# Starting the high parts of the weights 4 and 248 bytes further in two of four ring slots

## The chip, the cores and the metric

The kernel runs on one core of a Trainium2 chip. The metric is the device time of one execution in microseconds, the median of several runs. The kernel before took 1588.19 us (three runs, 1588.19 to 1588.33).

## What is computed

One layer of a streaming encoder block on a 256 x 2048 float32 input: a normed input is multiplied by `w_in` (2048 x 7680), the product feeds a gated spatial branch and a windowed attention branch, both go through output projections and `w_o`, and a gated MLP with a short causal convolution follows.

```
h = rms_norm(x, ln_pre_mix);  proj = h @ w_in
y_a = gmlp_branch(u, v_sg, ...) @ w_a_out;  y_b = swa_branch(q, k, v, ...) @ w_b_out
x = x + rms_norm((gate_a * y_a + gate_b * y_b) @ w_o, ln_post_mix)
up = rms_norm(x, ln_pre_ffn) @ w_up                    # 2048 x 16384
x = x + rms_norm((gelu(conv(gate)) * conv(val)) @ w_down, ln_post_ffn)
```

## The kernel before

Every large product is made from split operands. A float32 value is written as a high part (rounded to the type `F32R`) and a low part (what the rounding left), and three of the four products of the parts are summed: high by high, high by low and low by high.

**The flow of weights.** SyncE loads 1 MB units of weights into `raw` (four units of 2048 columns per partition). Each unit is two halves of 1024 columns. ScalarE rounds a half into `w_hi` (`split`, L454) and VectorE writes the rest into `w_lo` (`split`, L862). Both tensors are rings of four slots, and half h of a turn uses slot h modulo 4. ScalarE may overwrite a slot once TensorE has counted the half up on `half_used`; TensorE starts on a half once `hi_ready` or `lo_ready` says so.

**Two kinds of stages.** In the feature-major stages the weights are the stationary operand and the activations in `actT` the moving one. These are q, k, v and u, the gates, the two branch outputs, and the up-projection. A half has eight blocks of 128 x 128 weights. `by_hi` (L1494) loads a block of the high part and multiplies it with 512 columns (both parts of 256 tokens); `by_lo` (L1498) loads the same block of the low part and multiplies it with 256 columns (the high part alone). I call the first a wide matmul and the second a narrow one. `pair_a` works through two halves: 16 wide and 16 narrow matmuls. In `group_turn` the pairs alternate: halves 0 and 1 go wide first, then narrow; halves 2 and 3 go narrow first (`lo_first`), then wide. So a block of 64 matmuls reads, by slot: wide 0, wide 1, narrow 0, narrow 1, narrow 2, narrow 3, wide 2, wide 3, and then wide 0 again. There are 88 such blocks, in 44 turns. In `y_turn` (8 blocks of 64) every pair goes wide first. In the other stages (`half_b`, L1585, `half_v`, L1635, `last_halves`, L1598, and `seven_products`, L1778) the weights or forms of them are the moving operand. The first turn of the up-projection reads the high parts through `half_a` (L1509 and L1514), which the change leaves at the start of the slot.

**Where the parts lie.** A slot of `w_hi` is 1024 columns (4096 bytes per partition), and each of its blocks starts at a multiple of 512 bytes from the tensor's start. A slot of `w_lo` is 1152 columns (4608 bytes) wide, and in the feature-major stages the low part begins 64, 32, 16 and 128 bytes into slots 0 to 3 (`LO_SHIFT`, in columns 16, 8, 4, 32). `actT` comes behind them, and each of its rows begins at a multiple of 2048 bytes from its own start.

Of the kernel before, what the change touches and what calls it, by code (L numbers as in the profile page):

```python
# [6 lines left out]
ALU = mybir.AluOpType  # L7
ACT = mybir.ActivationFunctionType
AX = mybir.AxisListType
F32 = mybir.dt.float32  # L10
F32R = mybir.dt.float32r

P = 128
# [22 lines left out]
HALF = UNIT // 2  # L36
RAW = 4
RING = 4
# [24 lines left out]
def block_program(nc, x, x_t, pre_gains, w_in, ln_v_g, ln_v_b, w_spatial, b_spatial, rel_bias, sinks, w_a_out, w_b_out,  # L63
# [10 lines left out]
    with ExitStack() as ctx:  # L74
        def sb(name, shape, dt=F32):
            return ctx.enter_context(nc.sbuf_tensor(name, shape, dt))

        def sem(name):
            return ctx.enter_context(nc.semaphore(name))


        raw = sb("raw", [P, RAW, UNIT])
        w_hi = sb("w_hi", [P, RING, HALF], F32R)
        w_lo_padded = sb("w_lo", [P, RING, HALF + P], F32R)
        w_lo = w_lo_padded[:, :, 0:HALF]
        LO_SHIFT = (16, 8, 4, 32)
        w_lo_shifted = [w_lo_padded[:, slot, shift:shift + HALF] for slot, shift in enumerate(LO_SHIFT)]
# [93 lines left out]
        ps = ctx.enter_context(nc.psum_tensor("ps", [P, 8, 512], F32))  # L181
# [17 lines left out]
        hi_ready = sem("hi_ready")  # L199
        lo_ready = sem("lo_ready")  # L200
# [242 lines left out]

        @block.scalar
        def _(act):
            def split(m, h, fresh=False, free=None):

                if fresh and h == 2:
                    act.wait_ge(third_half_landed, 16)
                else:  # L450
                    act.wait_ge(raw_landed[h // 2], 16 * m + 16)
                if not fresh:
                    act.wait_ge(half_used, 8 * m + (h - RING + 1 if free is None else free))
                act.activation(w_hi[:, h % RING, :], raw[:, h // 2, h % 2 * HALF:(h % 2 + 1) * HALF], ACT.Copy)\  # L454
                   .then_inc(hi_ready, 1)

            def split_xs(m, h, src, free=None):

                act.wait_ge(half_used, 8 * m + (h - RING + 1 if free is None else free))
                act.activation(xs[:, h % RING, 0, :], src, ACT.Copy)  # L460
                split(m, h, free=free)

            def copy_out(g, bank, used):
                act.wait_ge(half_used, used)
# [4 lines left out]
            def split_x(k):  # L469
                for i, (k0, k1) in enumerate(XPIECES):  # L470
                    if k0 == k:
                        act.wait_ge(x_landed[i], 16)
                act.activation(actT[:, k, 0, :], xT[:, k, :], ACT.Copy, scale=gvec[:, 0, k:k + 1]).then_inc(hi_split, 1)
# [21 lines left out]
            def square(src, junk, col, done_sem=None):  # L495
                act.activation(junk, src, ACT.Square, accum_out=stat[:, col:col + 1]).then_inc(sq_done, 1)

            def root(col, t, before):
                act.wait_ge(ms_done, before + t + 1)
                act.activation(stat[:, ROOT + col + t:ROOT + col + t + 1], stat[:, col + t:col + t + 1], ACT.Sqrt)\  # L500
                   .then_inc(rt_done, 1)
# [17 lines left out]
            act.wait_ge(small["gains"], 16)  # L519
            for h in (2, 3):  # L520
                split_x(h)
                split(0, h, fresh=True)


            for h, k in ((4, 4), (5, None), (6, 6), (7, None)):
                if k is not None:
                    split_x(k)
                    split_x(k + 1)
                split(0, h)
            for h, k in ((0, 8), (1, 10), (2, 12), (3, 14), (4, None), (5, None), (6, None), (7, None)):  # L530
                if k is not None:
                    split_x(k)
                    split_x(k + 1)
                split(1, h)
                if h in (3, 4):
                    act.wait_ge(x_rows_landed, 16)
                    if h == 4:
                        act.wait_ge(sq_done, 1)
                    square(xn[:, h - 3, :], xs[:].rearrange("p r a s -> p (r a s)"), MIX_IN + h - 3)
                if h == 5:  # L540
                    for t in range(T):
                        root(MIX_IN, t, 0)

            for i in range((N_U - N_QKV) // 8):
                m = i + N_QKV // 8
# [34 lines left out]
            m = N_U // 8  # L580
# [166 lines left out]
            for i in range(2):  # L747
                m = N_WO // 8 + 2 + i
# [10 lines left out]
            m = N_UP // 8  # L759
# [8 lines left out]
            act.wait_ge(half_used, N_UP)  # L768
            square(ps[:, 3, :], junk_mix[:, T + 1, 512:SW], LAST_SQ[0])
            root(MIX_OUT, 1, 2 * T)  # L770
            split(m, 2)
            split_first_rows(1, 0, 1)
            split(m, 3)
            split_rows(1, 4, 1)
            split(m, 4)
            split(m, 5)
            split_rows(1, 4, 2)
            split(m, 6)
            act.wait_ge(x1_done, T * (D // XC - 1) + 2)
            square(x1[:, 0, :], junk_x1[:, 0, :], FFN_IN)  # L780
            split_rows(1, 4, 3)
            split(m, 7)
            act.wait_ge(x1_done, T * (D // XC) + 1)
            square(x1[:, 1, :], junk_x1[:, 1, :], FFN_IN + 1)
            for t in range(T):
# [69 lines left out]

        @block.vector
        def _(dve):
            def split(m, h, shifted=True):

                dve.wait_ge(hi_ready, 8 * m + (h + 1))  # L860
                lo = w_lo_shifted[h % RING] if shifted else w_lo[:, h % RING, :]
                dve.tensor_tensor(lo, raw[:, h // 2, h % 2 * HALF:(h % 2 + 1) * HALF],  # L862
                                  w_hi[:, h % RING, :].bitcast(F32), ALU.subtract).then_inc(lo_ready, 1)

            def split_xs(m, h, src):

                dve.wait_ge(hi_ready, 8 * m + (h + 1))
                dve.tensor_tensor(xs[:, h % RING, 1, :], src, xs[:, h % RING, 0, :].bitcast(F32), ALU.subtract)
                split(m, h, shifted=False)

            def add_out(g, bank, dst):
                dve.wait_ge(copied, g + 1)
# [59 lines left out]
            for k in (0, 1):  # L932
                dve.wait_ge(x_landed[k], 16)
                dve.tensor_scalar(actT[:, k, 0, :], xT[:, k, :], gvec[:, 0, k:k + 1], None, ALU.mult).then_inc(first_hi, 1)
                if k == 0:
                    split_x(0)
                    split(0, 0, shifted=False)
            split_x(1)
            split(0, 1, shifted=False)
            for h in (2, 3):  # L940
                split_x(h)
                split(0, h, shifted=False)
            for h, k in ((4, 4), (5, None), (6, 6), (7, None)):
                if k is not None:
                    split_x(k)
                    split_x(k + 1)
                split(0, h, shifted=False)
            for h, k in ((0, 8), (1, 10), (2, 12), (3, 14), (4, None), (5, None), (6, None), (7, None)):
                if k is not None:
                    split_x(k)  # L950
                    split_x(k + 1)
                split(1, h, shifted=False)
                if h == 4:
                    for t in range(T):
                        mean_square(MIX_IN, D, t, sq_done, t + 1)
                if h == 5:
                    for t in range(T):
                        recip(MIX_IN, t, 0)
                        col = RECIP + MIX_IN + t
                        dve.tensor_copy(rrep[:, t, :], stat[:, col:col + 1].broadcast_to([P, P])).then_inc(rrep_done, 1)  # L960
                if h == 6:
                    dve.wait_ge(small["relb"], 16)
                    dve.tensor_copy(relperm[0:BUCKETS].rearrange("p (k a b) -> p k a b", a=2, b=2),
                                    relb[:].rearrange("p (k b a) -> p k a b", a=2, b=2)).then_inc(rb_perm, 1)
# [4 lines left out]
            for i in range((N_U - N_QKV) // 8):  # L969
                m = i + N_QKV // 8  # L970
# [28 lines left out]
            m = N_U // 8  # L999
# [271 lines left out]
            for i in range(2):  # L1271
                m = N_WO // 8 + 2 + i
# [11 lines left out]
            m = N_UP // 8  # L1284
# [50 lines left out]
            residual(1, 1)  # L1335
            last_out(1, x1[:, 1, SW:D], gain[:, SW:D], sq_done, 4 * T + 1)
            split_rows(1, KD + 2, 1)
            split(m, 2, shifted=False)
            split(m, 3, shifted=False)
            residual(2, 0)  # L1340
            residual(2, 1)
            split_rows(1, KD + 2, 2)
            split(m, 4, shifted=False)
            residual(3, 0)
            residual(3, 1)
            split(m, 5, shifted=False)
            split_rows(1, KD + 2, 3)
            split(m, 6, shifted=False)
            split(m, 7, shifted=False)
            for t in range(T):  # L1350
                mean_square(FFN_IN, D, t, sq_done, 4 * T + t + 2)
            for t in range(T):
# [138 lines left out]
        @block.tensor  # L1491
        def _(pe):
            def by_hi(h, at, k, c, bank, start, stop):
                return pe.matmul(ps[:, bank + c, :], w_hi[:, h % RING, at:at + P],  # L1494
                                 actT[:, k, :, :].rearrange("p a s -> p (a s)"), start=start, stop=stop)

            def by_lo(h, at, k, c, bank, start, stop):
# [338 lines left out]
            m = N_UP // 8  # L1836
# [88 lines left out]
```

## Time and profile before

| | |
|---|---|
| median of the runs | 1588.19 us |
| the profiled execution, its own time | 1588.61 us |
| its span, first to last instruction | 1586.8 us |
| TensorE matmul busy | 1577.7 us, 99% |
| TensorE weight load busy | 1367.8 us, 86% |
| VectorE busy | 1260.4 us, 79% |
| ScalarE busy | 828.1 us, 52% |
| granted TensorE clock, mean | 0.999 |

A matmul's busy time runs past the start of the next one, since they are pipelined. The time that a matmul costs is therefore read as the step from its start to the start of the next. In the chain of work that ended last, consecutive matmuls of one line stand as one piece with its duration and their number, and duration over number is the mean step. Durations there have two decimals, so a piece is known to about 10 ns.

### The profile page before, as it was taken

Reading aid. Unit: us, or ns where it says so; the run is one execution under the profiler, and the core shown is the slowest. Engines: PE = TensorE matmul, PEld = TensorE weight load, DVE = VectorE, ACT = ScalarE, POOL = GpSimd, SP = SyncE. Lnnn points to the kernel's source line nnn. Section 1 sums busy time; section 2 is a strip of 40 time slices with the busy share of each in tenths; the row PEclk is TensorE's granted clock in tenths of the full one; section 3 lists DMA queues with packets and bytes.
Section 4 is the critical chain, followed back from the end, with each engine's and each line's share of the span. In section 5 each row is a group of like instructions: output and inputs, shape, how many; then the busy total and the mean of one; then the engine's idle time right before and its main releaser. Section 6 shows DMA issues by size and latency. Waiting matters only on the chain.

```text
span 1586.8 us, 24342 instructions
## 1 busy us (share of the span) xinstructions
PE 1577.7 (99%) x8652; PEld 1367.8 (86%) x8652; DVE 1260.4 (79%) x1836; ACT 828.1 (52%) x1124; POOL 1.9 (0%) x12
## 2 busy tenths in 40 slices
PE   9999999999999999999999999999999999999998
PEld 8888888888888888888888888888888888888886
DVE  6556677677797788777787777877778899989999
ACT  6544544456565654444444444444444575766664
POOL 0000000000000000000000000000000000000000
PEclk9999999999999999999999999999999999999999
DMA  9895455556566465556555566655666555555552
GB/s 371 267 232 190 160 185 163 181 160 203 194 241 217 152 210 187 186 185 200 190 190 185 185 197 190 195 185 185 195 189 198 199 208 207 208 198 200 185 212 106
DMA packets 234946, 313.15 MB, mean 197 GB/s; under 512 B 5360, under 2 KB 209808, under 8 KB 234000
## 3 DMA queue, kind: packets, MB, share of 16 engines
q1 hardware_dynamic: 231056, 306.44, 58.5%
q10 hardware_dynamic: 3840, 6.05, 1.5%
q8 instruction: 32, 0.52, 0.1%
q14 instruction: 18, 0.15, 0.0%
HBM read 309.58 MB, written 2.88 MB: 197 GB/s over the span
## 4 chain that ended last, share of the span: by engine, by line
PE 96%; DVE 4%; issue 0%; ACT 0%; DVEq 0%
PE ps L1494 44%; PE ps L1498 23%; PE ps L1585 15%; PE ps L1778 6%; PE ps L1635 3%; PE ps L1598 1%; DVE actT L1189 1%; DVE w_lo L1189 1%; PE ps L1509 1%; PE ps L1514 0%; DVE arena L1177 0%; PE ps L1724 0%; PE ps L1705 0%; PE ps L1657 0%; PE ps L1717 0%
## 5 line engine op out<-in xcount | busy, mean ns | idle before, releaser
L1494 PE MATMUL ps<-actT,w_hi 128*128 128x512 f32 x3072 | 715.4, 390 | 0.0
L454 ACT ACTIVATE w_hi<-raw 128x1024 fp32r<-128x1024 f32 x420 | 433.4, 1056 | 509.0 <-PE ps L1494 256.9
L862 DVE TENSOR_TENSOR w_lo<-raw,w_hi 128x1024 fp32r<-128x1024 f32 x422 | 506.1, 1223 | 236.8 <-ACT w_hi L454 234.5
L1494 PEld LDWEIGHTS ps<-actT,w_hi 128*128 128x128 f32 x3072 | 569.4, 188 | 113.0 <-issue 0.2
L1498 PEld LDWEIGHTS ps<-actT,w_lo 128*128 128x128 f32 x3072 | 378.2, 188 | 9.9 <-issue 1.7
L1498 PE MATMUL ps<-actT,w_lo 128*128 128x256 f32 x3072 | 384.4, 281 | 0.0
L1585 PE MATMUL ps<-w_hi,xs 128*128 128x512 f32 x832 | 226.6, 389 | 0.0
L1585 PEld LDWEIGHTS ps<-w_hi,xs 128*128 128x128 f32 x832 | 156.1, 188 | 32.4
L1585 PE MATMUL ps<-w_lo,xs 128*128 128x512 f32 x416 | 128.1, 389 | 0.0
L1189 DVE TENSOR_TENSOR w_lo<-raw,w_hi 128x1024 fp32r<-128x1024 f32 x96 | 117.3, 1222 | 0.0
L1379 DVE SCALAR_TENSOR_TENSOR arena<-arena,convw 128x256 f32<-128x256 f32 x256 | 106.8, 480 | 0.0
L713 ACT ACTIVATE w_hi<-raw 128x1024 fp32r<-128x1024 f32 x96 | 100.4, 1046 | 0.0
L1585 PEld LDWEIGHTS ps<-w_lo,xs 128*128 128x128 f32 x416 | 78.1, 188 | 16.3
L1778 PE MATMUL ps<-actT 128*128 128x512 f32 x288 | 81.0, 389 | 0.1
L691 ACT ACTIVATE actT<-raw 128x1024 fp32r<-128x1024 f32 x24 | 25.4, 1060 | 99.0 <-PE ps L1778 99.0
L873 DVE TENSOR_TENSOR arena<-ps,arena 128x512 f32<-128x512 f32 (+1 forms) x106 | 72.5, 684 | 1.5 <-ACT arena L467 1.4
L1778 PE MATMUL ps<-actT,a_parts 128*128 128x512 f32 x216 | 64.6, 389 | 0.0
L1778 PEld LDWEIGHTS ps<-actT 128*128 128x128 f32 x288 | 54.0, 188 | 11.8 <-DVE actT L1189 0.6
L467 ACT ACTIVATE arena<-ps 128x512 f32<-128x512 f32 x106 | 61.3, 579 | 2.9 <-PE ps L1514 1.4
L1189 DVE TENSOR_TENSOR actT<-arena,actT 128x1024 fp32r<-128x1024 f32 (+2 forms) x52 | 59.8, 1161 | 0.0
L711 ACT ACTIVATE xs<-arena 128x256 fp32r<-128x256 f32 x96 | 38.7, 403 | 24.7 <-PE ps L1585 13.8
L1367 DVE TENSOR_TENSOR arena<-arena,rrow 128x512 f32<-128x512 f32 x64 | 44.3, 692 | 6.5
(181 smaller groups left out, 935.7 us busy)
## 6 DMA issues: line engine op xcount, KB each, us to landing
raw<-in_w_up_dram SPq DMA_DIRECT2D x128, 1024.0 KB, 5.5
raw<-in_w_down_dram SPq DMA_DIRECT2D x64, 1024.0 KB, 5.2
raw<-in_w_in_dram SPq DMA_DIRECT2D x58, 1024.0 KB, 5.2
raw<-in_w_o_dram SPq DMA_DIRECT2D x16, 1024.0 KB, 5.3
raw<-in_w_a_out_dram SPq DMA_DIRECT2D x8, 1024.0 KB, 5.3
raw<-in_w_b_out_dram SPq DMA_DIRECT2D x8, 1024.0 KB, 5.2
arena<-in_x_dram SPq DMA_DIRECT2D x1, 2048.0 KB, 17.1
arena<-in_x_dram ACTq DMA_DIRECT2D x2, 1024.0 KB, 6.1
```

Source lines behind the costliest of these rows:

```text
L454: act.activation(w_hi[:, h % RING, :], raw[:, h // 2, h % 2 * HALF:(h % 2 + 1) * HALF], ACT.Copy)\
L467: act.activation(lo_part, ps[:, bank:bank + 2, S:2 * S], ACT.Copy).then_inc(copied, 1)
L713: act.activation(w_hi[:, slot, :], raw[:, unit.slot, j * HALF:(j + 1) * HALF], ACT.Copy).then_inc(hi_ready, 1)
L862: dve.tensor_tensor(lo, raw[:, h // 2, h % 2 * HALF:(h % 2 + 1) * HALF], w_hi[:, h % RING, :].bitcast(F32), ALU.subtract).then_inc(lo_read ...
L873: dve.tensor_tensor(dst, ps[:, bank:bank + 2, 0:S], lo_part, ALU.add).then_inc(summed, 1)
L1189: return dve.tensor_tensor(lo, full, hi.bitcast(F32), ALU.subtract)
L1379: dve.scalar_tensor_tensor(out=dst[:, a, :], in0=src[:, a, i:i + S], scalar=w(i, a), in1=dst[:, a, :], op0=ALU.mult, op1=ALU.add).then_inc ...
L1494: return pe.matmul(ps[:, bank + c, :], w_hi[:, h % RING, at:at + P], actT[:, k, :, :].rearrange("p a s -> p (a s)"), start=start, stop=stop)
L1498: return pe.matmul(ps[:, bank + c, 0:S], w_lo_shifted[h % RING][:, at:at + P], actT[:, k, 0, :], start=start, stop=stop)
L1585: ins = pe.matmul(ps[:, bank + 2 * t + c, :], xpart[:, tokens], wpart[:, slot, c * 512:(c + 1) * 512], start=(first and xpart is x_hi and ...
L1635: ins = pe.matmul(ps[:, 4 + 2 * t + c, :], xpart[:, t * P:(t + 1) * P], wpart[:, slot, c * 512:(c + 1) * 512], start=(k == 0 and xpart is ...
L1778: ins = pe.matmul(ps[:, bank, :], x[x_part], y[y_part], start=(unit.first and alone and x_part + y_part == 0), stop=(unit.last and alone a ...
```

## The change

`w_hi` becomes 1152 columns wide per slot, like `w_lo`. In the feature-major stages the high part then begins at column 0, 0, 1 and 62 of slots 0 to 3, that is 0, 0, 4 and 248 bytes further on. ScalarE writes there, VectorE reads there, and TensorE loads its stationary blocks from there. All three address a half as 8 blocks of 128 columns, which is the same run of addresses as before. In the other stages, and for the first turn of the up-projection, everything stays at the start of the slot (`padded=False` for ScalarE, `feature_major=False` for VectorE, the new name of `shifted=False`). What is allocated behind `w_hi` moves by 2048 bytes, and slot n of `w_hi` by 512 n bytes.

```diff
-        w_hi = sb("w_hi", [P, RING, HALF], F32R)
+        w_hi_padded = sb("w_hi", [P, RING, HALF + P], F32R)
+        w_hi = w_hi_padded[:, :, 0:HALF]
+        HI_SHIFT = (0, 0, 1, 62)
+        w_hi_blocks = [w_hi_padded[:, slot, shift:shift + HALF].rearrange("p (b c) -> p b c", c=P)
+                       for slot, shift in enumerate(HI_SHIFT)]
...
-            def split(m, h, fresh=False, free=None):
+            def split(m, h, fresh=False, free=None, padded=True):
...
-                act.activation(w_hi[:, h % RING, :], raw[:, h // 2, h % 2 * HALF:(h % 2 + 1) * HALF], ACT.Copy)\
-                   .then_inc(hi_ready, 1)
+                full, hi = raw[:, h // 2, h % 2 * HALF:(h % 2 + 1) * HALF], w_hi[:, h % RING, :]
+                if padded:
+                    full, hi = full.rearrange("p (b c) -> p b c", c=P), w_hi_blocks[h % RING]
+                act.activation(hi, full, ACT.Copy).then_inc(hi_ready, 1)
...
-            def split(m, h, shifted=True):
+            def split(m, h, feature_major=True):
...
-                lo = w_lo_shifted[h % RING] if shifted else w_lo[:, h % RING, :]
-                dve.tensor_tensor(lo, raw[:, h // 2, h % 2 * HALF:(h % 2 + 1) * HALF],
-                                  w_hi[:, h % RING, :].bitcast(F32), ALU.subtract).then_inc(lo_ready, 1)
+                full, hi = raw[:, h // 2, h % 2 * HALF:(h % 2 + 1) * HALF], w_hi[:, h % RING, :].bitcast(F32)
+                lo = w_lo[:, h % RING, :]
+                if feature_major:
+                    full, hi = full.rearrange("p (b c) -> p b c", c=P), w_hi_blocks[h % RING].bitcast(F32)
+                    lo = w_lo_shifted[h % RING].rearrange("p (b c) -> p b c", c=P)
+                dve.tensor_tensor(lo, full, hi, ALU.subtract).then_inc(lo_ready, 1)
...
             def by_hi(h, at, k, c, bank, start, stop):
-                return pe.matmul(ps[:, bank + c, :], w_hi[:, h % RING, at:at + P],
+                return pe.matmul(ps[:, bank + c, :], w_hi_blocks[h % RING][:, at // P, :],
                                  actT[:, k, :, :].rearrange("p a s -> p (a s)"), start=start, stop=stop)
```

## Rows read from the trace of the kernel before

**Rows 1.** The page: busy time, share of the span, instructions, by engine.
```profile
PE 1577.7 (99%) x8652; PEld 1367.8 (86%) x8652; DVE 1260.4 (79%) x1836; ACT 828.1 (52%) x1124; POOL 1.9 (0%) x12
```

**Rows 2.** Waits of TensorE, 61 to 1244 us: engine line <- releaser: us, times, longest.
```profile
PE ps L1824 <- DVE arena L1295: 0.5, 1, 0.5
PE ps L1526 <- DVE actT L919: 0.4, 1, 0.4
```

**Rows 3.** Chain that ended last, up-projection: start us, us, engine line, matmuls.
```profile
1008.89 7.26 PE ps L1494 x32
1016.15 3.78 PE ps L1498 x32
1019.93 7.26 PE ps L1494 x32
...
1030.97 7.26 PE ps L1494 x32
```

**Rows 4.** The chain cut to short windows around one change from narrow to wide.
```profile
1009.80 2.27 PE ps L1494 x10
...
1027.66 0.35 PE ps L1498 x3
...
1030.97 0.69 PE ps L1494 x3
```

**Rows 5.** The chain where weights are the moving operand (both parts).
```profile
477.30 43.52 PE ps L1585 x192
...
1244.36 21.76 PE ps L1585 x96
```

**Rows 6.** The chain in the branch outputs, every pair wide first.
```profile
379.60 3.65 PE ps L1494 x16
383.24 1.88 PE ps L1498 x16
385.13 3.64 PE ps L1494 x16
```

**Rows 7.** Groups by line and shape: busy us, mean ns of one, idle before.
```profile
L1494 PE MATMUL ps<-actT,w_hi 128*128 128x512 f32 x3072 | 715.4, 390 | 0.0
L1494 PEld LDWEIGHTS ps<-actT,w_hi 128*128 128x128 f32 x3072 | 569.4, 188 | 113.0 <-issue 0.2
L454 ACT ACTIVATE w_hi<-raw 128x1024 fp32r<-128x1024 f32 x420 | 433.4, 1056 | 509.0 <-PE ps L1494 256.9 <-PE ps L1498 238.7 <-DMA raw<-in_w_in_dram 10.8
L713 ACT ACTIVATE w_hi<-raw 128x1024 fp32r<-128x1024 f32 x96 | 100.4, 1046 | 0.0
L661 ACT ACTIVATE actT<-arena 128x1024 fp32r<-128x1024 f32 x4 | 4.0, 1051 | 1.6 <-DVE arena L1032 1.6
L1379 DVE SCALAR_TENSOR_TENSOR arena<-arena,convw 128x256 f32<-128x256 f32 x256 | 106.8, 480 | 0.0
L896 DVE SCALAR_TENSOR_TENSOR actT<-arena,gvec,actT 128x256 fp32r<-128x256 f32 x16 | 7.2, 480 | 0.1
```

**Rows 8.** Timeline, all engines: start us, us, engine line, [idle before <- releaser].
```profile
1032.83 1.06 ACT L454 ACTIVATE w_hi<-raw 128x1024 fp32r<-128x1024 f32 x1 [2.64 <-PE ps L1494]
1033.92 1.23 DVE L862 TENSOR_TENSOR w_lo<-raw,w_hi 128x1024 fp32r<-128x1024 f32 x1 [1.93 <-ACT w_hi L454]
1034.64 1.06 ACT L454 ACTIVATE w_hi<-raw 128x1024 fp32r<-128x1024 f32 x1 [0.75 <-PE ps L1494]
...
1035.74 1.23 DVE L862 TENSOR_TENSOR w_lo<-raw,w_hi 128x1024 fp32r<-128x1024 f32 x1 [0.59 <-ACT w_hi L454]
...
1038.07 3.94 PE L1498 MATMUL ps<-actT,w_lo 128*128 128x256 f32 x32
```

**Rows 9.** The chain in the up-projection's first turn, no part shifted (`half_a`).
```profile
546.25 0.95 PE ps L1514 x8
547.20 1.84 PE ps L1509 x8
...
549.40 0.36 PE ps L1514 x3
```

**Rows 10.** The chain in the opening matmuls, plain float32, 128 columns.
```profile
2.85 2.35 PE ps L1657 x11
```

## What I expected before the kernel ran

> **What bounds the kernel now.** I began with the page's busy times: TensorE is busy for 99% of the span, VectorE for 79%, ScalarE for 52% [rows 1]. A busy share says little for a pipelined engine, so I asked next for TensorE's waits. Over all feature-major stages, 1183 us long, it waits for another engine for 0.9 us in total [rows 2]. What is left to look at is the steps of the matmuls themselves, and they come out of the chain of work that ended last. In the up-projection it is an unbroken alternation of 32 wide matmuls in 7.26 us and 32 narrow ones in 3.78 us; two blocks later the starts (1008.89, 1019.93, 1030.97) have moved by exactly 11.04 us each time [rows 3]. So one block of 64 costs 11.04 us whatever the other engines do. Only a change in the steps of the matmuls can move the end.
>
> The reader should then compare the steps. Where the weights are the moving operand, 192 matmuls take 43.52 us and 96 take 21.76 us: 226.67 ns each, both parts alike [rows 5]. This is the even step of a matmul of 512 columns here. In the up-projection ten wide matmuls in the middle of a run take 2.27 us, the same even step, while the first three behind a narrow run take 0.69 us [rows 4] instead of 3 x 226.67 ns = 0.68 us. The narrow ones go at 3.78 / 32 = 118.1 ns [rows 3], with 0.35 us for three inside slot 0 [rows 4]. In the up-projection's first turn, where no low part is shifted, three narrow matmuls in the middle of a half take 0.36 us, 120 ns each [rows 9]. So the start of the stationary block does matter to the step of a narrow matmul: 120 ns with none of the parts shifted, about 118 ns with the low part shifted. What it does to a wide matmul no row shows, since every high part begins at a multiple of 512 bytes.
>
> **The change part by part.** It removes and adds no instruction and no wait. Its effects are these.
>
> (1) The wide matmuls of slots 2 and 3 load their blocks from addresses 4 and 248 bytes on. There are 16 in each of 96 blocks of 64, 1536 in all. Their weight load has a mean of 188 ns [rows 7] against a step of 226.67 ns, so it lies beside the matmul before it, and it ends in time even if it grows somewhat. Only the first load of slot 2 lies beside a narrow matmul. What can go is the unevenness behind it: 0.69 - 0.68 = 0.01 us per block [rows 4, 5] in the 88 blocks that turn from narrow to wide at slot 2, 0.88 us. The eight blocks of the branch outputs turn to wide at slot 2 and at slot 0; their runs of 16 take 3.65 and 3.64 us [rows 6] against 16 x 226.67 ns = 3.63 us, so at slot 2 there is 8 x 0.02 = 0.16 us. Together 1.04 us, if all of it goes. As these differences are at the limit of the view's two decimals, the ends are 0 and twice that, 2.1 us.
>
> (2) The steady step of these 1536 matmuls. The nearest rows give both signs. From above: the narrow matmuls lost about 1.9 ns (120 to 118.1 ns) with shifts of 16 to 128 bytes [rows 3, 9], and the same on 1536 wide ones is -2.9 us. From below: unshifted wide matmuls that are out of their even step take 1.84 us for eight [rows 9], 230 ns each, 3.3 ns more than the even step. On 1536 of them that is +5.1 us. I take zero, because the even step of 226.67 ns is the same for `w_hi` and `w_lo` as moving operand, for `xs` and for `w_hi` as stationary one, and from 477 to 1265 us [rows 4, 5]: it looks like a property of the 512 columns. Both ends stay for the range.
>
> (3) ScalarE writes and VectorE reads 4 bytes off. For VectorE the trace has the pair: the convolution reads its sources 4 and 8 bytes off in turn (L1379) and takes 480 ns, and the same operation on aligned ones (L896) takes 480 ns [rows 7]. So VectorE costs nothing more. For ScalarE no row has an odd start. Rounding a half is 1056 ns [rows 7]. The half that ScalarE takes up at 1032.83 us is complete when VectorE ends at 1033.92 + 1.23 = 1035.15 us, and TensorE needs it as the third half of the narrow run that starts at 1038.07, about 1.9 us into it: 4.8 us of slack; for the next half 1.1 us more is gone from VectorE's side and the slack is 3.9 us [rows 8]. A ScalarE twice as slow on two of the four slots would eat 1.06 us of that. Zero on the path, and zero from any rate that a row suggests. If that cover were gone, every microsecond of delay would stand once in each of 88 blocks.
>
> (4) The 8 x 128 form of the accesses. ScalarE's copy of four rows of 256 with gaps takes 1051 ns against 1046 and 1056 ns for the flat ones [rows 7]: nothing.
>
> (5) The layout. `w_lo`, `actT` and `xs` move together by 2048 bytes, so the narrow matmuls keep their relative addresses; the slots of `w_hi` come to lie 4608 bytes apart, as those of `w_lo` do, and as moving operands the two give one even step [rows 5]. I take zero. If against this all 3072 narrow matmuls fell back to 120 ns, that would be +5.8 us, and I leave that outside.
>
> The sum: 1588.61 us of the profiled execution (1586.8 us of span and 1.8 us around it) less 1.0 us. Against the median of 1588.19 us it is **1587.2 us**.
>
> The Trainium skill, "TensorE: Matmul & The Clock Gate", section "Step-by-step: what each phase is for", says that TensorE has two independent read ports, and that "Loading the next tile's weights doesn't steal SBUF read bandwidth from the running matmul". By that rule the address of a stationary block could matter to nothing, and the sum would be 1588.2 us. The trace speaks against it, by the 120 and 118 ns of the narrow matmuls. The same page, section "Back-to-back issue gap", gives a warm step of N/2.4 + 2.5 ns, 215.8 ns for 512 columns by its formula, where the rows have 226.67 ns. An estimate from that page would therefore leave 11 ns per matmul to be won by someone; on 1536 matmuls it would be 16.7 us.
>
> **The rivals.** *Nothing happens* (the shift doesn't do what it is put there for). The even step doesn't depend on the start, and the 10 ns behind the narrow run belong to the switch from one kind to the other, not to the address. For it: the same unevenness stands behind narrow runs of every stage, unshifted ones too [rows 9]. Time 1588.2 us.
>
> *The shift works on the wide ones as on the narrow ones.* -2.9 us from (2) and -1.0 us from (1): 1584.3 us. For it: it is the one effect of a shift that the trace has. Against it: a narrow matmul is near the length of a weight load, and a wide one is not.
>
> *The excess over the columns' own time goes.* Eleven plain matmuls took 2.35 us, 213.6 ns each [rows 10], for 128 columns that pass four times, which is as many column passes as 512. A wide matmul without its extra 13 ns on 1536 would be 20 us: about 1568 us. Nothing says that the start of the block is what keeps these 13 ns there.
>
> *Slower: the shifted halves lose the even step, and the next aligned ones must find it again.* The wide matmuls of the up-projection's first turn show what being out of step costs: 3.3 ns on each of eight [rows 9]. If slots 2 and 3 never find an even step with odd starts, that is 1536 x 3.3 = 5.1 us, and a return to step in the first wide half behind them another 8 x 3.3 = 26 ns in 96 blocks, 2.5 us, less nothing won at the turn: up to 1595.8 us, and about 1593 us if half of the return is paid. It decides from the point where a shifted wide matmul is slower by more than 0.7 ns on the mean (1.0 us over 1536).
>
> **How the numbers follow.** The unevenness goes in whole or in part, with the even step kept: 0.42, 1587.2 us with 1586.1 to 1588.2 as its own range. Nothing: 0.15. The wide ones gain as the narrow ones: 0.23, 1584.3. The large gain: 0.05. Slower: 0.15, 1593. The range of 1583.5 to 1591.5 us holds the first three cases and the lesser half of the last, and leaves out the large gain and the full loss. 0.2%, which is about what a measurement of this kernel can tell from no change, is 3.2 us. Faster by more takes the third and fourth case, 0.28; slower by more 0.15; within 0.57.
>
> **What would show it.** Right: in the chain, wide runs of 32 in 7.25 to 7.26 us with the first three in 0.68 us, narrow runs still in 3.78 us, blocks 11.03 us apart, and the waits of TensorE unchanged. Step (1) is wrong if the first three still take 0.69 us. Step (2) is wrong if ten wide matmuls of slots 2 and 3 take anything but 2.27 us, while those of slots 0 and 1 don't change. Step (3) is wrong if L454 has a second duration, (4) if slots 0 and 1 have a longer one too, and (5) if the narrow run moves from 3.78 us or the runs of L1585 from 226.67 ns. The prediction fails as a whole if the spacing of the blocks is under 11.00 or over 11.08 us.

## The result, and the profile after

The changed kernel took **1597.75 us** (three runs, 1597.48 to 1597.9) against 1588.19: a ratio of 1.0058, with a 95% interval of 1.0045 to 1.0072. It is slower by 0.6%, and it lies outside my range, which ended at 1591.5 us. The profiled execution took 1597.9 us, with a span of 1596.1 us where the kernel before has 1586.8. In the new code the lines have moved: the wide matmuls are L1503 (they were L1494), the narrow ones L1507 (L1498), ScalarE's rounding is L461 (L454), VectorE's subtraction L872 (L862).

The page first, then the groups by line (busy us, mean ns of one, idle before), as [rows 1] and [rows 7]:

```profile
PE 1586.9 (99%) x8652; PEld 1367.9 (86%) x8652; DVE 1260.5 (79%) x1836; ACT 828.2 (52%) x1124; POOL 1.9 (0%) x12
```
```profile
L1503 PE MATMUL ps<-actT,w_hi 128*128 128x512 f32 x3072 | 725.1, 393 | 0.0
L1503 PEld LDWEIGHTS ps<-actT,w_hi 128*128 128x128 f32 x3072 | 569.4, 188 | 122.3 <-issue 0.2
L872 DVE TENSOR_TENSOR w_lo<-raw,w_hi 128x1024 fp32r<-128x1024 f32 x422 | 506.2, 1223 | 245.5 <-ACT w_hi L461 243.2 <-ACT w_hi L520 1.6 <-ACT w_hi L523 0.6
L461 ACT ACTIVATE w_hi<-raw 128x1024 fp32r<-128x1024 f32 x420 | 433.5, 1056 | 517.4 <-PE ps L1503 263.1 <-PE ps L1507 241.1 <-DMA raw<-in_w_in_dram 11.6
L1507 PE MATMUL ps<-actT,w_lo 128*128 128x256 f32 x3072 | 384.2, 281 | 0.0
L1594 PE MATMUL ps<-w_hi,xs 128*128 128x512 f32 x832 | 226.7, 389 | 0.0
```

All engines but TensorE's matmuls are where they were. The whole of the growth of TensorE is in one row: 725.1 us for the wide matmuls where it was 715.4, so +9.7 us. The narrow ones (384.2 against 384.4 before) and the matmuls that read weights as moving operand (226.7) have not moved. The weight load that got the new addresses still shows 188 ns, so its own row hides what happened; only the steps of the matmuls show it.

The waits of TensorE for other engines, 61 to 1252 us, are the two of [rows 2]:

```profile
PE ps L1833 <- DVE arena L1304: 0.5, 1, 0.5
PE ps L1535 <- DVE actT L928: 0.4, 1, 0.4
```

The chain that ended last, up-projection (start us, us, engine line, matmuls), as [rows 3]:

```profile
1004.80 7.37 PE ps L1503 x32
1012.16 3.77 PE ps L1507 x32
1015.93 7.37 PE ps L1503 x32
...
1038.21 7.37 PE ps L1503 x32
```

Narrow runs are as they were, wide runs take 7.37 us in place of 7.26. Three blocks go from 1004.80 to 1038.21 us, 11.137 us each, so 0.097 us more than 11.04; times 88 blocks that is 8.5 us. Cut into eights, the wide run from 1027.08 us reads (slots 2, 3, 0 and 1 in turn; same columns):

```profile
1027.08 1.85 PE ps L1503 x8
1028.93 1.86 PE ps L1503 x8
1030.79 1.83 PE ps L1503 x8
1032.63 1.81 PE ps L1503 x8
```

and the same four pieces of the kernel before:

```profile
1030.97 1.82 PE ps L1494 x8
1032.79 1.81 PE ps L1494 x8
1034.60 1.81 PE ps L1494 x8
1036.42 1.81 PE ps L1494 x8
```

Each half is 0.03, 0.05, 0.02 and 0.00 us longer: the two shifted halves, and then the first **unshifted** one behind them. In the branch outputs (as [rows 6]) only the run on slots 2 and 3 is longer, 3.72 us against 3.64:

```profile
382.11 3.65 PE ps L1503 x16
385.75 1.89 PE ps L1507 x16
387.64 3.72 PE ps L1503 x16
```

With 0.01 us more in the narrow run before it, these eight blocks give 8 x 0.09 = 0.7 us. 8.5 + 0.7 = 9.2 us of the 9.3 us by which the span has grown. The time is found; what is left is its cause.

Two decimals are coarse for this, so I also took the start of every single matmul from the trace and averaged each of the 63 steps over some 60 equal blocks of the up-projection. In the kernel before, the wide matmuls go at 226.67 ns but for the first few behind the narrow run. After, those of slot 2 have a mean of 231.8 ns, those of slot 3 233.2 ns, and the first eight of slot 0 take 21 ns more in all until 226.67 ns is found again. "Single starts" below means this working.

### The profile page after: what moved, and what is told of

It is laid out like the page before. It is cut to its first block, busy times and chain, and to the rows that moved or that the text cites. A ratio compares the mean times of both kernels' runs of the same rounds, so it can differ in the third digit from the quotient of the medians.

```text
span 1596.1 us, 24342 instructions
## 1 busy us (share of the span) xinstructions
PE 1586.9 (99%) x8652; PEld 1367.9 (86%) x8652; DVE 1260.5 (79%) x1836; ACT 828.2 (52%) x1124; POOL 1.9 (0%) x12
## 4 chain that ended last, share of the span: by engine, by line
PE 96%; DVE 4%; issue 0%; ACT 0%; DVEq 0%
PE ps L1503 44%; PE ps L1507 23%; PE ps L1594 15%; PE ps L1787 6%; PE ps L1644 3%; PE ps L1607 1%; DVE actT L1198 1%; DVE w_lo L1198 1%; PE ps L1518 1%; PE ps L1523 0%; DVE arena L1186 0%; PE ps L1733 0%; PE ps L1714 0%; PE ps L1666 0%; PE ps L1726 0%
## 5 line engine op out<-in xcount | busy, mean ns | idle before, releaser
L1503 PE MATMUL ps<-actT,w_hi 128*128 128x512 f32 x3072 | 725.1, 393 | 0.0
L461 ACT ACTIVATE w_hi<-raw 128x1024 fp32r<-128x1024 f32 x420 | 433.5, 1056 | 517.4 <-PE ps L1503 263.1
L872 DVE TENSOR_TENSOR w_lo<-raw,w_hi 128x1024 fp32r<-128x1024 f32 x422 | 506.2, 1223 | 245.5 <-ACT w_hi L461 243.2
L1503 PEld LDWEIGHTS ps<-actT,w_hi 128*128 128x128 f32 x3072 | 569.4, 188 | 122.3 <-issue 0.2
L1507 PEld LDWEIGHTS ps<-actT,w_lo 128*128 128x128 f32 x3072 | 378.2, 188 | 9.9 <-issue 1.7
L1507 PE MATMUL ps<-actT,w_lo 128*128 128x256 f32 x3072 | 384.2, 281 | 0.0
L1594 PE MATMUL ps<-w_hi,xs 128*128 128x512 f32 x832 | 226.7, 389 | 0.0
L1787 PEld LDWEIGHTS ps<-actT 128*128 128x128 f32 x288 | 54.0, 188 | 11.7 <-DVE actT L1198 0.6
```

The lines of the kernel that those rows point to most:

```text
L461: act.activation(hi, full, ACT.Copy).then_inc(hi_ready, 1)
L872: dve.tensor_tensor(lo, full, hi, ALU.subtract).then_inc(lo_ready, 1)
L1503: return pe.matmul(ps[:, bank + c, :], w_hi_blocks[h % RING][:, at // P, :], actT[:, k, :, :].rearrange("p a s -> p (a s)"), start=start, ...
L1507: return pe.matmul(ps[:, bank + c, 0:S], w_lo_shifted[h % RING][:, at:at + P], actT[:, k, 0, :], start=start, stop=stop)
L1594: ins = pe.matmul(ps[:, bank + 2 * t + c, :], xpart[:, tokens], wpart[:, slot, c * 512:(c + 1) * 512], start=(first and xpart is x_hi and ...
L1787: ins = pe.matmul(ps[:, bank, :], x[x_part], y[y_part], start=(unit.first and alone and x_part + y_part == 0), stop=(unit.last and alone a ...
```

## The experiments

Each is the changed kernel with other starts; every kernel does all of the computation. The kernel before took 1588.08 to 1588.36 us (medians) on the same chips, and its single executions 1587.92 to 1588.51 us. Unless more is said, a time below is that of one execution, so differences of half a microsecond say nothing.

### Which part of the change costs

```diff
-        HI_SHIFT = (0, 0, 1, 62)
+        HI_SHIFT = (0, 0, 0, 0)       # pad_only: the layout and the 8 x 128 form alone
+        HI_SHIFT = (0, 0, 1, 0)       # slot2_only: 4 bytes
+        HI_SHIFT = (0, 0, 0, 62)      # slot3_only: 248 bytes
```

> The wider slots of w_hi and the 8 x 128 form of the accesses, with no part of w_hi shifted. Theory (the start address of the stationary block inside its 512 bytes costs the even step): about 1588.2 us, wide runs of 32 in 7.26 us as before, 226.67 ns a step in all four slots. Rival (the layout costs it: slots 4608 bytes apart, or w_lo and actT moved by 2048 bytes): near 1597.8 us, wide runs of 32 in 7.37 us.

> Only slot 2 starts 4 bytes further. Theory (each shifted half loses its even step, and the next aligned half pays to find it again): the wide matmuls of slot 2 take about 231.8 ns each as after the change, and slot 3, now aligned, pays the return of about 20 ns and then goes at 226.67 ns. Block of 64: 11.04 + 8 x 0.005 + 0.02 = 11.10 us, time 1588.2 + 96 x 0.05 = 1593.0 us. Rival (only the 248 bytes of slot 3 are bad, and slot 2 suffers nothing by its own 4 bytes): 1588 us, block 11.04 us.

> Only slot 3 starts 248 bytes further. Theory: slot 2 goes back to 227.9 ns mean of its eight (two uneven steps behind the narrow run, as before the change), slot 3 takes about 233 ns each, slot 0 behind it pays about 20 ns: block 11.04 + 8 x 0.0065 + 0.02 = 11.11 us, time about 1595 us. Rival (the two shifts act only together): near 1588 us. The excess of slot2_only and slot3_only over before should add up to the 9.6 us of the change plus one more return of 96 x 0.02 = 1.9 us.

Measured: **1588.51**, **1593.1** and **1595.85 us**. The chain of the first is that of the kernel before:

```profile
1030.88 7.26 PE ps L1503 x32
1038.14 3.78 PE ps L1507 x32
```

So wider slots, moved tensors and the three-dimensional form cost nothing that can be told from noise (0.4 us), and the starts cost the rest. With slot 2 alone shifted, its eight take 1.85 us and the next, unshifted eight of slot 3 take 1.84 (from 1034.50 us); with slot 3 alone shifted it is slot 3 and then slot 0 (the last two of three lines):

```profile
1034.50 1.85 PE ps L1503 x8
1036.35 1.84 PE ps L1503 x8
1038.18 1.81 PE ps L1503 x8
```
```profile
1036.62 1.83 PE ps L1503 x8
1038.45 1.86 PE ps L1503 x8
1040.32 1.83 PE ps L1503 x8
```

Each shifted half pays for itself and for a return. The two prices are +5.0 and +7.8 us, 12.8 in all, where the change cost 9.6. With both shifted, the return inside slot 3 is saved in each of 96 blocks: 24.8 ns by the single starts of slot2_only, 2.4 of the 3.2 us. The remaining 0.8 us is not accounted for; each of the two prices is the difference of two single executions.

### Is it an odd start, a 16-byte line, or a larger unit?

A start that isn't a multiple of 16 or of 128 bytes might be what hurts. Three pairs of starts tell these units apart.

```diff
-        HI_SHIFT = (0, 0, 1, 62)
+        HI_SHIFT = (0, 0, 4, 60)      # whole_lines: 16 and 240 bytes
+        HI_SHIFT = (0, 0, 32, 96)     # steps_of_128: 128 and 384 bytes
+        HI_SHIFT = (0, 0, 128, 64)    # steps_of_256_512: 512 and 256 bytes
```

> Slots 2 and 3 start 16 and 240 bytes further, both multiples of 16 bytes, in place of 4 and 248. Theory A (it is the start off a multiple of 16 bytes that costs): slots 2 and 3 keep 226.67 ns or less, time 1586 to 1588.5 us. Theory B (any start that is not a multiple of a larger unit, 128 bytes or more, loses the even step, as the narrow matmuls change with starts of 16 to 64 bytes): slots 2 and 3 take a step other than 226.67 ns; if as bad as the odd starts, near 1597 us.

> Slots 2 and 3 of w_hi start 128 and 384 bytes further. Theory (what counts is the start within 128 bytes): the even step of 226.67 ns stays in all slots, 1588 us. Rival (within 512 bytes, or any shift at all): slots 2 and 3 go at 229 to 233 ns as with 16 and 240 bytes, time 1593 to 1598 us.

> Slot 2 starts 512 bytes further, slot 3 256 bytes. Theory (what counts is where the 512 bytes of a block start within 512 bytes): slot 2 goes as before the change, 227.9 ns mean of its eight; slot 3 goes at 229 to 233 ns, and slot 0 pays a return of about 20 ns, as in slot3_only: time 1593 to 1596 us. Rival 1 (the unit is 256 bytes): both slots as before, 1588 us. Rival 2 (the distance from the ordinary place counts): both slots at 229 to 233 ns, 1597 us.

Measured: **1594.39**, **1594.81** and **1588.47 us**. The runs of 32 wide matmuls, first with 16 and 240 bytes, then with 128 and 384, then with 512 and 256:

```profile
1035.46 7.33 PE ps L1503 x32
```
```profile
1035.85 7.33 PE ps L1503 x32
```
```profile
1030.78 7.26 PE ps L1503 x32
```

Multiples of 16 and of 128 bytes are slow like the odd ones, 256 and 512 are as fast as no shift. So a unit of 16 bytes falls, one of 128 bytes too, and for 256 bytes I had expected a loss: there the rival held. Of the units tried it is **256 bytes**, counted from the start of the tensor; where the tensor itself lies the trace doesn't tell. The odd starts of the change are only some 3 us worse than the even ones that miss the unit.

### Does the start count, or the jump from one start to another?

In all these the shifted slots stand between unshifted ones. So all four get the same shift:

```diff
-        HI_SHIFT = (0, 0, 1, 62)
+        HI_SHIFT = (4, 4, 4, 4)       # all_16_bytes
```

> All four slots of w_hi start 16 bytes further, so that no wide matmul follows one with another start. Theory A (the start itself denies the even step): the 32 wide matmuls of a block stay near 279 cycles of 1.2 GHz, 232.5 ns, all along, and the time is about 1588.2 + 3072 x 0.0058 = 1606 us. Theory B (only a change of start costs, over some eight to ten matmuls): the first ten are uneven and the others go at 226.67 ns: 1588.2 + 88 x 0.05 = about 1593 us.

Measured: **1605.69 us**, +17.4.

```profile
1029.38 3.76 PE ps L1507 x32
1033.14 7.47 PE ps L1503 x32
```

7.47 / 32 = 233.4 ns for every wide matmul. There is no jump among these 32, so a jump isn't needed: with this start alone they stay off the even step, 6.7 ns each. (That such a start doesn't always do so comes at the end.) In the single starts six of the narrow ones in slot 0 now go at 113.3 ns, one after another, which no row of the kernel before has. That asked for a look at the narrow ones.

### The narrow matmuls

```diff
-        HI_SHIFT = (0, 0, 1, 62)
+        HI_SHIFT = (0, 0, 0, 0)       # lo_unshifted, lo_64_bytes
+        HI_SHIFT = (16, 16, 16, 16)   # all_64_bytes
-        LO_SHIFT = (16, 8, 4, 32)
+        LO_SHIFT = (0, 0, 0, 0)       # lo_unshifted
+        LO_SHIFT = (16, 16, 16, 16)   # lo_64_bytes, all_64_bytes
```

> No part shifted, neither high nor low (the wider slots of w_hi stay, which cost nothing). Theory (one cause for both: with aligned starts matmuls fall into an even step, 226.67 ns for a wide one and 120.0 ns for a narrow one, and out of it a wide one takes longer while a narrow one takes less): narrow runs of 32 in 3.84 us in place of 3.78, wide runs of 32 in 7.25 us, block 11.09 us, time 1588.2 + 96 x 0.055 = about 1593 us. Rival (narrow and wide have nothing to do with each other, and the shifts of the low parts do little): 1588 us, block 11.04 us.

> High and low parts of all four slots start 64 bytes further. Theory (a start off 512 bytes denies a wide matmul its even step of 226.67 ns, whatever the start): wide ones near 233 ns, and the narrow ones, once on the grid of 6.67 ns on which the even matmuls start, at 113.3 ns as six of them did in all_16_bytes: 32 x 233 + 32 x 114 = 11.10 us a block, time about 1594 us. Rival (64 bytes is as good for a wide matmul as for a narrow one, and its step falls below 226.67 ns): below 1588 us.

> High parts in the ordinary place, low parts of all four slots 64 bytes further. In the kernel before, the narrow matmuls of slot 0, which start there, go through 141, 141 and 142 cycles of 1.2 GHz in turn. Theory (entered from an aligned wide run, the first narrow one falls off the grid by one cycle and the run goes round these three): 117.8 ns a step all through, narrow run 3.77 us, block 11.03 us, time 1587 us within 1.5. Rival (with one start throughout, the run finds the step of 113.3 ns after some matmuls): narrow run about 3.65 us, time about 1577 us.

Measured: **1594.45**, **1593.18** and **1587.72 us**. The chains, low parts unshifted; then everything 64 bytes on; then only the low parts 64 bytes on:

```profile
1031.59 3.83 PE ps L1507 x32
1035.42 7.28 PE ps L1503 x32
```
```profile
1030.79 3.63 PE ps L1507 x32
1034.42 7.46 PE ps L1503 x32
```
```profile
1026.12 3.77 PE ps L1507 x32
1029.89 7.28 PE ps L1503 x32
```

The low parts' shifts of the kernel before are thus worth 6.2 us. For the narrow ones a start off 256 bytes is good where it is bad for the wide ones: aligned, they keep an even step of 120.0 ns (3.83 / 32 = 119.7), and off it they can go at 3.63 / 32 = 113.4 ns. But they do so only in the second kernel. In the third, with the same low parts, they rotate at 117.8 ns. What differs is how they are entered. The single starts show it where the wide ones before them are even: if the first narrow block, which loads beside the last wide matmul, is aligned (lo_unshifted), that wide matmul keeps 226.67 ns and the first narrow one takes 113.3 ns; if the block is off (lo_64_bytes), the wide one is 0.8 ns early, the first narrow one takes 118 ns, and the later ones keep the phase in which they began.

### The handover repaired

If that is right, the first narrow block of a run must be aligned and all later ones not. The first low block of slot 0 goes to the start of the slot by a VectorE instruction of its own, the other seven stay 64 bytes on:

```diff
+        HI_SHIFT = (0, 0, 0, 0);  LO_SHIFT = (16, 16, 16, 16)    # first_block_aligned
...
+                    if h % RING == 0:
+                        dve.tensor_tensor(w_lo_padded[:, 0, 0:P], full[:, 0, :], hi[:, 0, :], ALU.subtract)
+                        lo, full, hi = lo[:, 1:8, :], full[:, 1:8, :], hi[:, 1:8, :]
...
+                block = w_lo_padded[:, 0, 0:P] if h % RING == 0 and at == 0 else w_lo_shifted[h % RING][:, at:at + P]
```

> As lo_64_bytes, but the first low block of slot 0 lies at the start of the slot; VectorE writes it by an instruction of its own, and the other seven 64 bytes further. Theory (an aligned wide run hands over on the grid if the next block is aligned, as in lo_unshifted, and from there a block 64 bytes off goes at 136 cycles, 113.3 ns, as in all_16_bytes): all 32 narrow ones of a block at 113.3 ns, narrow run 3.63 us, block 10.88 to 10.92 us, time 1588.2 - 96 x 0.13 to 0.16 = about 1574 us. Rival (the 113.3 ns of all_16_bytes hung on its high parts being 16 bytes off): as lo_64_bytes, 1587 us.

Measured: **1576.55 us** (four runs, 1576.45 to 1576.96), a ratio of 0.9927 (0.991 to 0.9944) to the kernel before.

```profile
1028.44 3.63 PE ps L1511 x32
1032.06 7.28 PE ps L1506 x32
```

The narrow run went from 3.78 to 3.63 us: 88 x 0.15 = 13.2 us, of which the wide run gives 88 x 0.02 = 1.8 back; 11.4 of the 11.7 us measured. I had expected about 1574 us; the blocks came as expected (10.91 us), but the sum counted 0.13 to 0.16 us in 96 of them. The wide run's 0.02 us are its first eight (1.84 us), which are entered from a narrow run with an aligned block. So the other handover gets the opposite of what the low part got, the first high block of slot 2 off the unit and all others on it:

```diff
+        HI_SHIFT = (0, 0, P, 0);  LO_SHIFT = (16, 16, 16, 16)    # both_handovers
...
+                if padded and h % RING == 2:
+                    act.activation(w_hi_padded[:, 2, 16:16 + P], full[:, 0, :], ACT.Copy)
+                    full, hi = full[:, 1:8, :], hi[:, 1:8, :]
...
+                block = w_hi_padded[:, 2, 16:16 + P] if h % RING == 2 and at == 0 else w_hi_blocks[h % RING][:, at // P, :]
```

> As first_block_aligned, and the first high block of slot 2 lies 64 bytes further (the other seven 512 bytes further, which costs nothing), written by an instruction of its own on ScalarE. Theory (the last narrow matmul keeps to the grid if the next block is 64 bytes off too, and the wide one behind it goes even if its next block is aligned): the 32 cycles behind the narrow run go, 26.7 ns in each of 88 blocks and 8 of the branch outputs, wide run of 32 in 7.25 us, time 1576.55 - 2.5 = 1574.0 us. Rival (a change from narrow to wide costs the return to step whatever the block's start): 1576.6 us.

Measured: **1574.09 us** (five runs, 1573.59 to 1574.45), a ratio of 0.9911 (0.9897 to 0.9924). It beats both kernels.

```profile
1026.79 3.63 PE ps L1518 x32
1030.41 7.25 PE ps L1513 x32
1037.67 3.63 PE ps L1518 x32
```

The price stands in the groups by line (slot 2's high part in two instructions; slots 0 and 2 on VectorE in two):

```profile
L462 ACT ACTIVATE w_hi<-raw 128x128 fp32r<-128x128 f32 x96 | 29.7, 310 | 205.9 <-PE ps L1513 187.0 <-PE ps L1518 17.9 <-DMA raw<-in_w_in_dram 1.0
L464 ACT ACTIVATE w_hi<-raw 128x896 fp32r<-128x896 f32 x96 | 90.0, 937 | 0.0
L881 DVE TENSOR_TENSOR w_lo<-raw,w_hi 128x896 fp32r<-128x896 f32 x192 | 208.0, 1084 | 0.0
```

310 + 937 - 1056 = 191 ns more of ScalarE in each block, and some 150 ns more of VectorE for each of its two split halves. It lies in their slack: TensorE still waits for other engines for 0.9 us only.

### Is it the stationary operand alone?

By then I held that only the stationary block's start matters. `actT`, the moving operand of the wide and narrow matmuls, is put 16 bytes on, with and without the weights.

```diff
-        actT = sb("actT", [P, KD, 2, S], F32R)
+        actT_padded = sb("actT", [P, KD * 2 * S + P], F32R)
+        actT = actT_padded[:, 4:4 + KD * 2 * S].rearrange("p (k a s) -> p k a s", a=2, s=S)
...
+        HI_SHIFT = (4, 4, 4, 4);  LO_SHIFT = (20, 12, 8, 36)    # both_16_bytes: all operands by 16 bytes
+        HI_SHIFT = (0, 0, 0, 0)                                 # moving_16_bytes: actT alone
```

> As all_16_bytes, but actT, the moving operand, starts 16 bytes further as well, and so do the low parts (80, 48, 32 and 144 bytes). Theory A (the start of the stationary block against that of the moving operand counts): the wide matmuls are back at 226.67 ns, the narrow ones at 118.1 ns, the feature-major blocks at 11.04 us; the stages where actT or aligned slots meet the other kind lose a little (half_v, half_a, parts of the seven products): 1589 to 1592 us. Theory B (the start of the stationary block alone counts): as all_16_bytes, within 3 us of it.

> Only actT, the moving operand of the feature-major stages, starts 16 bytes further; every high part lies in its ordinary place, the low parts where the kernel before has them. Theory (the start of the stationary block alone decides): wide matmuls at 226.67 ns, time 1588 to 1590 us, where the stages that take their stationary blocks from actT (half_v, the seven products) lose up to 2.5 us. Rival (the moving operand's start counts as much, and both_16_bytes was slow because both were off): wide ones near 233 ns, about 1607 us.

Measured: **1607.85** and **1605.55 us**. That it is the distance between the operands that counts is out: with everything shifted alike it is the slowest kernel of all, and its wide run takes 7.45 us.

```profile
1033.29 7.45 PE ps L1504 x32
```

And my theory fell, for the moving operand's start alone costs about what the stationary one's does (1605.69). The wide run takes 7.42 us with `actT` alone shifted:

```profile
1031.13 7.42 PE ps L1504 x32
```

That the two totals are so near is in part chance. 7.42 / 32 = 231.8 ns is 5.1 ns over the even step, where all_16_bytes had 6.7; the rest comes from the narrow matmuls (3.79 us for 32) and from other stages that read `actT`.

## Why the prediction was wrong

**The bound** was right: nothing but the steps of the matmuls moved the end, and the block spacing carried the result as it was read. The spacing of 11.14 us is over the 11.08 at which I said that the prediction fails.

**Step (1), the unevenness at the turn**, fell. I took 1.04 us for it; the first half behind the narrow run became 0.03 us longer. The term also had a misread row in it: slot 2 of the branch outputs is the run of 3.64 us, so its share was 8 x 0.01 and not 8 x 0.02 us (0.96 us in all); the 3.65 us are slot 0's. The run both_handovers shows that there was something to win there (7.25 us), but by an off start of one block only, entered from narrow matmuls on their 113.3 ns step. The 4 bytes on all eight blocks took away more than they could give.

**Step (2), the steady step, is where the prediction failed.** I had bounded it by -2.9 and +5.1 us and took zero, "because the even step of 226.67 ns is the same for `w_hi` and `w_lo` as moving operand, for `xs` and for `w_hi` as stationary one". Each of those operands starts at a multiple of 512 bytes. Four equal rows said that the step doesn't depend on the tensor; on the start they said nothing, because it never varied. The one place where starts did vary, 120 against 118 ns in the narrow matmuls, said that they matter, and I had it in the text. pad_only, slot2_only and slot3_only tie the loss to this step, and the single starts give its true size: 5.1 ns on each wide matmul of slot 2 and 6.5 of slot 3, 768 x 5.1 + 768 x 6.5 = 8.9 us, and 0.021 us x 88 = 1.8 us of returns, less what those wide matmuls had before (the uneven start of slot 2, 0.01 us x 96 = 1.0 us): 9.7 us, near the 9.6 measured.

**The rival "slower"** was the right mechanism, with both its parts: shifted halves out of step, and a return in the next aligned half. Its terms were mis-sized. It took 3.3 ns per matmul from [rows 9], 1.84 us for eight; but those eight are aligned blocks on their way back, a few late and the rest even, and a mean over them isn't a steady state. A row of blocks that stay out of step didn't exist in the trace. Its return of 26 ns was good (21 measured), though it comes in 88 blocks and not in 96: in the branch outputs narrow matmuls follow the shifted halves. With 6.5 ns in place of 3.3 its upper end would have been above 1597.75 us. Its middle was a wrong sum: with half of the return paid, its terms give 1588.2 + 5.1 + 1.3 = 1594.6 us, not 1593. I gave it 0.15 and ended the range short of it, although its own decision point, 0.7 ns, was small beside every effect of a start that the trace had.

**Steps (3), (4) and (5)** held. ScalarE's and VectorE's rows are the same to the nanosecond (1056 and 1223 ns), no second duration appears in L461, and pad_only is the kernel before within 0.4 us.

The rivals in which the wide ones gain, or in which the 13 ns over the columns' own time go, fell: no start made eight wide matmuls faster than 226.67 ns each. The one gain that was to be had lay in the narrow ones (120.0 to 113.3 ns), where I hadn't looked, as the change didn't touch them.

Of the Trainium skill I had cited "TensorE: Matmul & The Clock Gate", section "Step-by-step: what each phase is for", by which loading the next weights takes no read bandwidth from the running matmul. No run here agrees in the sense in which I used it, that the address of a stationary block matters to nothing: moving that address alone changes the wide step from 226.67 to 233.4 ns (all_16_bytes). Whether a read port has to do with it, no run tells.

## What to carry to other kernels

When rows agree, ask which quantity varied among them: equality over tensors that all start alike says nothing on starts. Where TensorE waits for nobody, read its steps from start to start, in groups of eight, one for each buffer slot. A price taken from a transient is no bound for a steady state; and a rival whose decision point is smaller than the effects already seen deserves more than a small chance.

## What the hardware showed that I had not expected

- In the up-projection a wide matmul (512 columns) held 226.67 ns only where the stationary block started at a multiple of 256 bytes of a tensor laid as here (0, 256 and 512 did; 4, 16, 64, 128, 240, 248 and 384 bytes did not, each in the place where it was tried) and the moving operand was not shifted (16 bytes is the only shift tried for it); otherwise it took 229 ns (240 bytes) to 233.4 ns on the mean of eight.
- A narrow one (256 columns) was the other way round: 120.0 ns aligned (lo_unshifted), 113.3 ns with its blocks 64 bytes off, if entered in phase (first_block_aligned), and 117.8 ns if not (lo_64_bytes).
- The phase is carried over. One block of 128 x 128 at another start, at each of two turns, is worth 13.6 us of this kernel (1587.72 us of lo_64_bytes to 1574.09); against the kernel before it is 14.3 us or 0.9%. The even steps, 226.67, 120.0 and 113.3 ns, are 34, 18 and 17 times 6.67 ns. That TensorE falls into step with something of that period is only argued, not shown.
- What stays open: an off start doesn't always lose the even step. In `half_v` the stationary operand is `actT`, and with the same starts in both kernels (16 bytes on, the moving `w_hi` at the slot's start) it ran at 34.54 / 152 = 227.2 ns in moving_16_bytes and at 35.24 / 151 = 233.4 ns in both_16_bytes:

```profile
14.86 34.54 PE ps L1645 x152
```
```profile
14.88 35.24 PE ps L1645 x151
```

The mean of 227.2 ns hides a change of step. In moving_16_bytes this stage began at 8.64 / 37 = 233.5 ns, had one step of 255 ns (from 16.56 us), and then went at 31.06 / 137 = 226.7 ns to its end:

```profile
7.85 8.64 PE ps L1645 x37
16.98 31.06 PE ps L1645 x137
```

So off operands can hold the even step too, once they are on it, and the starts alone don't decide. Aligned operands came back to the even step in every run. In both_16_bytes two longer steps in this stage, of 277 and 307 ns at 11.1 us, did not bring the even step. No run tests what decides it. The turn from narrow to wide at slot 0 in the branch outputs is still uneven in both_handovers and was not tried.
